# First mixer: SiLU from ScalarE's own table instead of tanh and a VectorE step, and a group's decay exponentials made together

## Chip, cores and metric

The kernel runs on one core of a Trainium2 chip. The metric is the device time of one execution in microseconds (us), the median of several runs. The engines are TensorE (PE in the profile; its weight loads are PEld), VectorE (DVE), ScalarE (ACT), GpSimd (POOL) and SyncE (SP), which issues the DMAs.

## What is computed

The reference is a chain of two transformer blocks over 272 (16 + 256), then 256 tokens with 1024 features. The change touches its first mixer alone, `ssd_mixer`: an input projection to 48 x 128 features, a causal convolution of four taps with SiLU, a chunked state recurrence for 8 groups of 4 heads over chunks of 16, 128 and 128 tokens, a gate by SiLU of `z`, a norm and an output projection:

```
z, xbc, dt = jnp.split(h @ w_in, ...)
xbc = jax.nn.silu(causal_depthwise_conv(xbc, conv_w, conv_b))
xs, b_in, c_in = jnp.split(xbc, ...)
...
decay = jnp.exp(jnp.where(causal, a_cs[..., :, None] - a_cs[..., None, :], -jnp.inf))
cb = jnp.einsum('bclgn,bcsgn->bcgls', c_c, b_c)
y_diag = jnp.einsum('bcgjls,bcsgjp->bclgjp', cb[:, :, :, None] * decay, xdt)
decay_to_end = jnp.exp(a_cs[..., -1:] - a_cs)
...
y_off = jnp.einsum('bclgn,bcgjpn->bclgjp', c_c, prev) * decay_from_start[..., None]
y = y + xs * d_skip
g = y * jax.nn.silu(z)
```

## The kernel before

All weights stream in through one ordered list of blocks, `PLAN`. A block is 128 output features: SP loads 512 KB into one of four `RAW` buffers, ACT rounds it to `WH` (`act_split`), DVE subtracts to get the remainder `WL` (`dve_split`), and PE multiplies with three matmuls for each of 8 chunks, 24 in all (`pe_block`). ACT makes `WH` three blocks ahead (`LEAD`), DVE makes `WL` two ahead (`LEAD_LO`).

The first mixer is the block "dt", then 48 blocks of the input projection, called block 0 to block 47 here, six to a group: two of x, one of b, one of c, two of z. Each engine runs a fixed, written-out program with a step for each block n, and executes it strictly in that order; only semaphores tie the engines together. In step n:

- ACT splits the weights of block n+3, starts the convolution of block n (`conv_base`, a scaled copy into `TMP`; not for z), and makes the tanh of block n-1, which waits for that block's third tap.
- DVE splits block n+2, makes the SiLU of block n-2 from its tanh (`dve_silu`, one scalar_tensor_tensor into `G6`), and adds the three taps of block n-1 (`dve_taps`).
- every engine then does its part of the recurrence (the "core") of the groups that are due: group g's core has 14 steps, and step k falls on n = 6g + 5 + k (`ssd_cores`).

In the core of group g, PE's `pe_prepare(g, i)` writes bank 3 for tile i: C.B, two transposes of x and, for the first two tiles, the transpose of B. DVE takes `xdt` from it, ACT copies the transposed B to `btk` (semaphore "bt"), and PE may write bank 3 again only after that: `pe_prepare(g, 1)` waits for the `btk` copy of tile 0. Then `act_prepare` makes the decays of the tile: an exponential of `ROWS` into `CE`, four Relu into `EE` (difference of two cumulated sums for each of four heads), and one exponential of `EE`. Tiles 0, 1 and 2 of group g are prepared in steps 6g+6, 6g+7 and 6g+10, and `pe_apply` uses them in steps 6g+8, 6g+10 and 6g+12. POOL multiplies `CE` with C. Step k = 12 of a group, two groups later in order, makes a logarithm and an exponential (`act_table`) and so loads another activation table.

PE's place in a bank is given back by the tap or, for a z block, by the SiLU of the block (`ssd_read`): block n waits for the reader of block n-3.

Of the kernel before, what the change touches and what calls it, by code (L numbers as in the profile page):

```python
# [5 lines left out]
ALU = mybir.AluOpType  # L6
# [5 lines left out]
T1 = 272  # L12
# [7 lines left out]
EXPS = "exp_and_others"  # L20

# [194 lines left out]
def build_program(nc, cpack, xin, memin, gains, W, out):  # L216
    with ExitStack() as ctx:
# [312 lines left out]
        EE = carve(2, 512)  # L530
        CE = carve(512)
        STA = carve(2, 256)

        ROWS = carve(2, 4, T1)
        decay_rows = nc.dram_tensor("decay_rows", [32, T1], F32, kind="Internal").ap()
        s_scanned = sem("s_decay_rows_stored")
        s_rows = [sem("s_decay_rows0"), sem("s_decay_rows1")]
        halved = sig("conv_halved")
# [5 lines left out]
        ident, tap, tanh, silu = sig("conv_base"), sig("conv_tap"), sig("tanh"), sig("silu")  # L544
# [25 lines left out]
        def ssd_cores(n):  # L570

            c = [(g, n - 6 * g - 5) for g in range(8) if 1 <= n - 6 * g - 5 <= 14]
            return c[::-1] if n < 50 else c

        def ssd_tile(g, i):
            o, L = TILES[i]
            return o, L, (3 * g + i) % 2

# [21 lines left out]
        def pe_prepare(q, g, i):  # L600
# [17 lines left out]
        def pe_apply(q, g, i):  # L618
            o, L, z = ssd_tile(g, i)
            yb, sbk = banks[5], banks[6]  # L620
            E4 = EE[:, z, :].rearrange("p (h l) -> p h l", h=4)
# [8 lines left out]
            for h in range(4):  # L630
                o_ = yb[64 * (h % 2):64 * (h % 2) + 64, 128 * (h // 2):128 * (h // 2) + L]
                t = q.matmul(o_, xdt[0:L, z, 64 * h:64 * h + 64], E4[0:L, h, 0:L], True, i == 0)
                if i:
                    t = q.matmul(o_, STA[:, i - 1, 64 * h:64 * h + 64], CE[:, 128 * h:128 * h + 128], False, True)
# [86 lines left out]
        def act_dt_core(q, k):  # L721
# [7 lines left out]
            else:  # L729
                for i, (o, L) in enumerate(TILES):  # L730
                    q.activation(acs[0:L, i, :], b[0:L, 64 * i:64 * i + 32], ACT.Copy).then_inc(*dta("acs", i))
                q.activation(dec[:, :], b[:, 96:128], ACT.Exp).then_inc(*dta("dec"))
                for i in range(2):
                    L = TILES[i][1]
                    q.wait_ge(*dtd["to_end", i])
                    q.activation(dte[0:L, i, :], dte[0:L, i, :], ACT.Exp).then_inc(*dta("dte", i))

        def act_prepare(q, g, i):
            o, L, z = ssd_tile(g, i)
            b = banks[3]  # L740
            E4 = EE[:, z, :].rearrange("p (h l) -> p h l", h=4)
            A4 = ROWS[:, g % 2, :, o:o + L]
# [14 lines left out]
            p = before(g, i, 2)  # L757
            if p is not None:
                q.wait_ge(*yps[p])
            for h in range(4):  # L760
                t = q.activation(E4[0:L, h, 0:L], A4[0:L, h, :], ACT.Relu, -1.0, acs[0:L, i, 4 * g + h:4 * g + h + 1])
            t.then_inc(*rel(g, i))
            q.wait_ge(*rel[g, i])
            q.activation(E4[0:L, :, 0:L], E4[0:L, :, 0:L], ACT.Exp, -1.0).then_inc(*dexp(g, i))

        def act_ssd_core(q, g, k):
            s = g % 2
            key = ("ssd", g)
            if k == 1:
# [9 lines left out]
            elif k == 5:  # L779
                act_prepare(q, g, 2)  # L780
# [28 lines left out]
        def act_ssd(q):  # L809
# [8 lines left out]
            for n in range(48):  # L818
                act_block(q, "ssd", 0, n, T1)
                if n % 6 < 4:  # L820
                    ch = ssd_channel(n)
                    q.wait_ge(*halved["b"])
# [53 lines left out]
        def dve_dt_core(q, k):  # L876
# [6 lines left out]
            else:  # L883
                q.wait_ge(*dta["dec"])
# [31 lines left out]
        def dve_weigh(q, g, i):  # L916
            o, L, z = ssd_tile(g, i)
            E4 = EE[:, z, :].rearrange("p (h l) -> p h l", h=4)
            q.wait_ge(*dexp[g, i])
# [2539 lines left out]
```

## Time and profile before

| what | value |
|---|---|
| median of 3 runs | 1629.4 us (1629.14 to 1630.18) |
| profiled execution | 1627.8 us |
| its span, first to last instruction | 1625.9 us |
| PE busy | 1604.5 us, 99% of the span |
| DVE busy | 1149.4 us, 71% |
| ACT busy | 963.5 us, 59% |
| POOL busy | 320.7 us, 20% |
| DMA | 161 GB/s in the mean |

The profiled execution's time is 1.9 us more than its span. Busy shares are means over stages; the first mixer lies between 11 us and about 255 us of the span. Matmuls are pipelined: a row's duration overlaps the next one's, so the distance between two starts tells the pace.

### The profile page before, as it was taken

The page shows a single profiled execution, that of the slowest core. Times are in us where ns is not written, and L with a number is a line of the kernel's source. Part 1 is how long each engine was busy: PE and PEld are TensorE (multiplying, and loading weights), DVE is VectorE, ACT ScalarE, POOL GpSimd, SP SyncE. Part 2 cuts the span into 40 slices and gives each one's busy share as a digit, 9 for nine tenths or more (in the row PEclk, how much of TensorE's full clock was granted, in tenths as well). Part 3 has the DMA queues.
Part 4 walks back from the last instruction along what each step waited for, and adds up shares of the span by engine and source line. Part 5 has one row for each costly group of instructions (what it writes and reads, how often), then busy time and mean ns, then how long its engine had stood idle before and what let it go on. Part 6 is the DMA issues. An engine that isn't in the chain of part 4 may idle for free.

```text
span 1625.9 us, 31615 instructions
## 1 busy us (share of the span) xinstructions
PE 1604.5 (99%) x12696; PEld 1545.1 (95%) x12696; DVE 1149.4 (71%) x1965; ACT 963.5 (59%) x1753; POOL 320.7 (20%) x291
## 2 busy tenths in 40 slices
PE   7999999999999999999999999999999999999998
PEld 7999999999998899999999999999999999999997
DVE  7999987555578765556776756766688767785655
ACT  7788876544456755544766645544466765664444
POOL 0001002234442232336311201000240111100000
PEclk9999999999999999999999999999999999999999
DMA  6544445555532356556545544555564445455553
GB/s 218 174 157 131 158 139 160 180 171 170 180 104 86 98 183 195 183 182 192 156 141 170 171 127 159 179 174 181 178 195 152 142 137 158 121 166 184 182 191 118
DMA packets 75792, 261.81 MB, mean 161 GB/s; under 512 B 8416, under 2 KB 11904, under 8 KB 75520
## 3 DMA queue, kind: packets, MB, share of 16 engines
q1 hardware_dynamic: 75648, 259.80, 51.1%
q8 instruction: 101, 1.65, 0.4%
q14 instruction: 43, 0.35, 0.1%
HBM read 258.68 MB, written 1.08 MB: 160 GB/s over the span
## 4 chain that ended last, share of the span: by engine, by line
PE 87%; DVE 5%; ACT 3%; issue 2%; POOL 2%; DMA 0%; DVEq 0%; SPq 0%; POOLq 0%; ACTq 0%
PE pb L156 86%; PE pb L159 2%; DVE WL L175 1%; POOL X L175 1%; DVE SCR L187 1%; DVE TMP L187 1%; ACT SCR L166 1%; ACT WH L165 1%; POOL SQ L175 1%; ACT HNH L165 0%; DVE SCR L175 0%; POOL SCR L175 0%; DVE HNL L187 0%; ACT SQ L165 0%; DVE MX L196 0%
## 5 line engine op out<-in xcount | busy, mean ns | idle before, releaser
L175 DVE TENSOR_TENSOR WL<-RAW,WH 128x1024 fp32r<-128x1024 f32 (+4 forms) x504 | 598.1, 1191 | 9.5 <-ACT WH L165 9.2
L165 ACT ACTIVATE WH<-RAW 128x1024 fp32r<-128x1024 f32 (+4 forms) x504 | 504.9, 1004 | 135.7 <-PE pb L156 135.2
L156 PE MATMUL pb<-HNH,WH 128*128 128x256 f32 (+1 forms) x1992 | 576.2, 289 | 1.5 <-issue 1.1
L156 PE MATMUL pb<-HNH,WL 128*128 128x256 f32 (+1 forms) x1992 | 564.8, 284 | 0.0
L156 PE MATMUL pb<-HNL,WH 128*128 128x256 f32 (+1 forms) x1992 | 564.6, 283 | 0.0
L156 PE MATMUL pb<-ASH,WH 128*128 128x256 f32 (+2 forms) x1392 | 400.3, 288 | 2.8 <-DVE WL L175 2.5
L156 PE MATMUL pb<-ASH,WL 128*128 128x256 f32 (+2 forms) x1392 | 394.9, 284 | 0.0
L156 PE MATMUL pb<-ASL,WH 128*128 128x256 f32 (+2 forms) x1392 | 394.3, 283 | 0.0
L156 PEld LDWEIGHTS pb<-HNH,WH 128*128 128x128 f32 x1992 | 375.7, 189 | 8.3 <-issue 3.2
L156 PEld LDWEIGHTS pb<-HNL,WH 128*128 128x128 f32 x1992 | 374.8, 188 | 2.0
L156 PEld LDWEIGHTS pb<-HNH,WL 128*128 128x128 f32 x1992 | 376.2, 189 | 0.0
L156 PEld LDWEIGHTS pb<-ASH,WH 128*128 128x128 f32 (+1 forms) x1392 | 261.9, 188 | 7.5 <-issue 5.1
L156 PEld LDWEIGHTS pb<-ASH,WL 128*128 128x128 f32 (+1 forms) x1392 | 262.1, 188 | 0.1
L156 PEld LDWEIGHTS pb<-ASL,WH 128*128 128x128 f32 (+1 forms) x1392 | 261.3, 188 | 0.7
L175 POOL TENSOR_TENSOR SQ<-SQ 128x256 f32<-128x256 f32 (+1 forms) x64 | 82.1, 1283 | 236.5 <-ACT SQ L165 236.3
L175 DVE TENSOR_TENSOR ASL<-TMP,ASH 128x256 fp32r<-128x256 f32 (+1 forms) x108 | 46.5, 430 | 108.8 <-ACT ASH L165 108.7
L156 PE MATMUL pb<-SCR 128*64 128x128 f32 (+10 forms) x880 | 119.3, 314 | 0.9 <-DVE SCR L187 0.8
L165 ACT ACTIVATE ASH<-TMP 128x256 fp32r<-128x256 f32 (+1 forms) x108 | 45.6, 422 | 114.6 <-DVE TMP L175 65.0
L175 POOL TENSOR_TENSOR X<-X,TMP 128x272 f32<-128x272 f32 (+1 forms) x64 | 96.3, 1505 | 79.5 <-DVE TMP L175 79.5
L156 PEld LDWEIGHTS pb<-SCR 128*64 128x64 f32 (+4 forms) x880 | 89.4, 160 | 20.4 <-issue 8.4
L175 POOL TENSOR_TENSOR SCR<-SCR 128x512 f32<-128x512 f32 (+2 forms) x36 | 44.6, 1247 | 310.9 <-DVE SCR L187 180.4
L165 ACT ACTIVATE TMP<-TMP 128x256 f32<-128x256 f32 (+1 forms) x84 | 35.4, 422 | 112.3 <-DVE TMP L187 111.9
(170 smaller groups left out, 1888.0 us busy)
## 6 DMA issues: line engine op xcount, KB each, us to landing
RAW<-in_w_gu SPq DMA_DIRECT2D x88, 512.0 KB, 4.2
RAW<-in_w_up SPq DMA_DIRECT2D x64, 512.0 KB, 3.7
RAW<-in_w_down SPq DMA_DIRECT2D x64, 512.0 KB, 3.6
RAW<-in_w_ssd SPq DMA_DIRECT2D x48, 512.0 KB, 3.6
RAW<-in_w_xkv SPq DMA_DIRECT2D x32, 512.0 KB, 4.2
RAW<-in_w_mlin SPq DMA_DIRECT2D x24, 512.0 KB, 3.6
RAW<-in_w_sbqkv SPq DMA_DIRECT2D x24, 512.0 KB, 3.6
RAW<-in_w_fd SPq DMA_DIRECT2D x22, 512.0 KB, 3.5
```

The costliest lines, as they stand in the source:

```text
L156: return self.eng.matmul(o, l, r, start=start, stop=stop, skip_group_check=skip) if self.eng else Nothing()
L159: return self.eng.transpose(o, i, ident) if self.eng else Nothing()
L165: return self.eng.activation(o, i, f, bias=bias, scale=scale)
L166: return self.eng.activation(o, i, f, bias=bias, scale=scale, accum_out=accum)
L175: return self.eng.tensor_tensor(o, a, b, op) if self.eng else Nothing()
L187: return self.eng.scalar_tensor_tensor(out=o, in0=a, scalar=s, in1=b, op0=op0, op1=op1)
```

## The change

SiLU is taken from ScalarE's Silu function, straight into `G6`. The tanh, the DVE step, the halving of the convolution's weights on POOL and the factor 0.5 at the gate go. The Relu go ahead of them: for g > 0 tile 1 in step k = -2 and tiles 0 and 2 in step k = -1, for g = 0 all three in step k = 0. For g = 0 the exponentials of `dec` and `dte` move there too, from step 3. `CE` and `EE` have two copies (by group parity), `ROWS` only one. POOL's products for both long tiles wait for a tap of block 6g+7.

```
         def ssd_cores(n):
-            c = [(g, n - 6 * g - 5) for g in range(8) if 1 <= n - 6 * g - 5 <= 14]
+            c = [(g, n - 6 * g - 5) for g in range(8) if -2 <= n - 6 * g - 5 <= 14]
...
         def pe_prepare(q, g, i):
-                q.wait_ge(*dta["dec"])
+                q.wait_ge(*dta["dec_log"])
...
         def act_prepare(q, g, i):
...
                 q.activation(btk[0:L, i, :], b[0:L, 384:512], ACT.Copy).then_inc(*btkd(g, i))
-            if i == 0:
-                q.wait_ge(s_rows[g % 2], 16 * (g // 2 + 1))
-            if i:
-                p = (g, 1) if i == 2 else (g - 1, 2)
-                if p[0] >= 0:
-                    q.wait_ge(*yps[p])
-                q.activation(CE[:, :].rearrange("p (h l) -> p h l", h=4), A4, ACT.Exp).then_inc(*cex(g, i))
...
-            q.wait_ge(*rel[g, i])
-            q.activation(E4[0:L, :, 0:L], E4[0:L, :, 0:L], ACT.Exp, -1.0).then_inc(*dexp(g, i))
+        def act_relu(q, g, i):
+            o, L = TILES[i]
+            q.wait_ge(s_rows, 16 * (g + 1))
+            if g > 1:
+                q.wait_ge(*yps[g - 2, i])
+            for h in range(4):
+                t = q.activation(decay(g, i)[:, h, :], ROWS[0:L, h, o:o + L], ACT.Relu, -1.0,
+                                 acs[0:L, i, 4 * g + h:4 * g + h + 1])
+            t.then_inc(*rel(g, i))
+        def act_decays(q, g):
+            q.table(LOGS)
+            if not g:
+                q.wait_ge(*dta["dec_log"])
+                q.activation(dec[:, :], dec[:, :], ACT.Exp).then_inc(*dta("dec"))
+                for i in range(2):
+                    L = TILES[i][1]
+                    q.wait_ge(*dtd["to_end", i])
+                    q.activation(dte[0:L, i, :], dte[0:L, i, :], ACT.Exp).then_inc(*dta("dte", i))
+            q.activation(CE[:, g % 2, :, :], ROWS[:, :, NMETA:T1], ACT.Exp).then_inc(*cex(g))
+            q.wait_ge(*rel[g, 0])
+            q.activation(decay(g, 0), decay(g, 0), ACT.Exp, -1.0).then_inc(*dexp(g, 0))
+            q.wait_ge(*rel[g, 2])
+            e = EE[:, g % 2, :, :]
+            q.activation(e, e, ACT.Exp, -1.0).then_inc(*dexp(g, 1))
...
         def act_ssd_core(q, g, k):
-            if k == 1:
+            if k == -2 and g:
+                act_relu(q, g, 1)
+            elif k == -1 and g:
+                act_relu(q, g, 0)
+                act_relu(q, g, 2)
+            elif k == 0:
+                if not g:
+                    for i in (1, 0, 2):
+                        act_relu(q, g, i)
+                act_decays(q, g)
+            elif k == 1:
                 act_prepare(q, g, 0)
...
         def act_ssd_item(q, n):
-            if n >= 2:
-                q.wait_ge(*silu[n - 2])
-            q.table(EXPS)
-            d = TMP[:, 3 + n % 2, 0:T1]
+            q.table(SILU)
+            if n >= 18:
+                q.wait_ge(*gated[n // 6 - 3])
             if n % 6 < 4:
                 q.wait_ge(*tap[n, 2])
-                q.activation(d, TMP[:, n % 3, 0:T1], ACT.Tanh).then_inc(*tanh(n))
+                v = TMP[:, n % 3, 0:T1]
             else:
                 q.wait_ge(*ssd_ready(n))
-                q.activation(d, ssd_source(n), ACT.Tanh, 0.5).then_inc(*tanh(n))
+                v = ssd_source(n)
+            q.activation(G6[:, n // 6 % 3, n % 6, :], v, ACT.Silu).then_inc(*silu(n))
...
-        def dve_silu(q, n):
-            q.stt(G6[:, n // 6 % 3, n % 6, :], TMP[:, 3 + n % 2, 0:T1], 1.0, v, ALU.add, ALU.mult).then_inc(*silu(n))
...
         def pool_ssd(q):
-            q.ts(cc("convw"), cc("convw"), 0.5, ALU.mult).then_inc(*halved("w"))
-            q.ts(cc("convb"), cc("convb"), 0.5, ALU.mult).then_inc(*halved("b"))
...
         def sync_rows(q, g):
-            if g < 2:
+            if g:
+                q.wait_ge(*cex[g - 1])
+            else:
                 q.wait_ge(s_scanned, 16)
-            else:
-                q.wait_ge(*rel[g - 2, 2])
```

The first place is ACT in steps 4 to 6, up to the `btk` copy of group 0's tile 0 (`SCR<-pb 16x128`). Names: `WH<-RAW` is a weight split, `TMP<-pb,cp` a `conv_base`, `TMP<-TMP` and `TMP<-SCR` a tanh. ACT before:

```order
L165 ACTIVATE WH<-RAW 128x1024 [waits block_done,s_raw0]
L165 ACTIVATE TMP<-TMP 128x272 [waits conv_tap,silu]
L165 ACTIVATE WH<-RAW 128x1024 [waits block_done,s_raw1]
L165 ACTIVATE TMP<-SCR 128x272 [waits evicted_dve,silu]
L165 ACTIVATE WH<-RAW 128x1024 [waits block_done,s_raw2]
L165 ACTIVATE TMP<-pb,cp 128x272 [waits silu,block_done]
L165 ACTIVATE TMP<-SCR 128x272 [waits evicted_dve]
L165 ACTIVATE SCR<-pb 16x128 [waits spare_state_rows,xdt]
```

ACT now, from the silu of block 3 to the same copy (the split and the silu of block 4 ahead of the Relu are left out here; they stand as before):

```order
L166 ACTIVATE SCR<-SCR 128x128 [waits s_decay_rows]
L166 ACTIVATE SCR<-SCR 128x128 x3
L166 ACTIVATE SCR<-SCR 16x16 x4
L166 ACTIVATE SCR<-SCR 128x128 x4
L173 ACT_TABLE_LOAD
L166 ACTIVATE SCR<-SCR 128x32 [waits dt_act]
L166 ACTIVATE SCR<-SCR 16x32 [waits dt_dve]
L166 ACTIVATE SCR<-SCR 128x32 [waits dt_dve]
L166 ACTIVATE SCR<-SCR 128x1024
L166 ACTIVATE SCR<-SCR 16x64 [waits decay_relu]
L166 ACTIVATE SCR<-SCR 128x1024 [waits decay_relu]
```

```order
L166 ACTIVATE WH<-RAW 128x1024 [waits block_done,s_raw2]
L166 ACTIVATE TMP<-pb,cp 128x272 [waits silu,block_done]
L173 ACT_TABLE_LOAD
L166 ACTIVATE SCR<-SCR 128x272 [waits evicted_dve]
L166 ACTIVATE SCR<-pb 16x128 [waits spare_state_rows,xdt]
```

Twelve Relu, six exponentials and two table loads now stand ahead of the copy, between the tanh (now silu) of block 4 and it.

The second place is ACT in the same two steps of a later group (g >= 2). Before:

```order
L165 ACTIVATE WH<-RAW 128x1024 [waits block_done,s_raw1]
L165 ACTIVATE TMP<-pb 128x272 [waits silu]
L172 ACT_TABLE_LOAD
L165 ACTIVATE Rbuf<-pb,cp 128x272 [waits squares_summed]
L165 ACTIVATE Rbuf<-Rbuf 128x272 [waits ln_of_sum]
L165 ACTIVATE WH<-RAW 128x1024 [waits block_done,s_raw2]
L165 ACTIVATE TMP<-pb,cp 128x272 [waits silu,block_done]
L172 ACT_TABLE_LOAD
L165 ACTIVATE TMP<-pb 128x272
L165 ACTIVATE SCR<-pb 16x128 [waits xdt]
```

Now:

```order
L166 ACTIVATE SCR<-pb 128x272
L173 ACT_TABLE_LOAD
L166 ACTIVATE SCR<-SCR 128x1024
L166 ACTIVATE SCR<-SCR 16x64 [waits decay_relu]
L166 ACTIVATE SCR<-SCR 128x1024 [waits decay_relu]
L166 ACTIVATE Rbuf<-pb,cp 128x272 [waits squares_summed]
L166 ACTIVATE Rbuf<-Rbuf 128x272 [waits ln_of_sum]
L166 ACTIVATE WH<-RAW 128x1024 [waits block_done,s_raw2]
L166 ACTIVATE TMP<-pb,cp 128x272 [waits silu,block_done]
L173 ACT_TABLE_LOAD
L166 ACTIVATE SCR<-pb 128x272
L166 ACTIVATE SCR<-pb 16x128 [waits xdt]
```

Here only the three exponentials came in between; the Relu stand one and two steps earlier, and the two table loads were there before.

The third place is what PE waits for at the beginning of group 0's core; its rows are the same before and now but for line numbers. `SCR 128x128 [waits bt]` is `pe_prepare(0, 1)`, after block 7:

```order
L156 MATMUL pb<-SCR 16x16 [waits silu,dt_act,dt_dve]
L159 MATMUL pb<-cp,SCR 16x128 x3
L156 MATMUL pb<-HNH,WH 128x272 [waits w_low,evicted_dve]
...
L156 MATMUL pb<-SCR 128x128 [waits bt]
L159 MATMUL pb<-cp,SCR 128x128 x3
L156 MATMUL pb<-HNH,WH 128x272 [waits w_low,evicted_dve]
```

Nothing moved on PE.

## Rows read from the trace of the kernel before

**Rows 1.** The page's busy line, and PE's waits from 10 to 60 us.

```profile
PE 1604.5 (99%) x12696; PEld 1545.1 (95%) x12696; DVE 1149.4 (71%) x1965; ACT 963.5 (59%) x1753; POOL 320.7 (20%) x291
...
PE pb L156 <- DVE WL L175: 1.1, 2, 0.7
PE pb L156 <- ACT SCR L165: 0.6, 1, 0.6
```

**Rows 2.** Timeline of PE, blocks 6 to 8: start, duration, idle before.

```profile
38.09 0.36 PE L156 MATMUL pb<-HNH,WH 128*128 128x272 f32 x1 [1.10 <-issue]
...
42.15 0.20 PE L156 MATMUL pb<-SCR 128*16 128x16 f32 x2 [0.81 <-DVE SCR L187]
...
42.54 0.37 PE L156 MATMUL pb<-HNH,WH 128*128 128x272 f32 x1
...
45.52 0.29 PE L156 MATMUL pb<-HNH,WL 128*128 128x272 f32 x1
45.64 0.38 PE L156 MATMUL pb<-SCR 128*128 128x128 f32 x2
...
46.11 0.37 PE L156 MATMUL pb<-HNH,WH 128*128 128x272 f32 x1
```

**Rows 3.** Timeline of PE around the preparation of tile 1, groups 4 and 5.

```profile
143.18 0.29 PE L156 MATMUL pb<-HNH,WL 128*128 128x272 f32 x1
...
143.89 0.39 PE L156 MATMUL pb<-HNH,WH 128*128 128x272 f32 x1
...
167.93 0.29 PE L156 MATMUL pb<-HNH,WL 128*128 128x272 f32 x1
...
168.93 0.39 PE L156 MATMUL pb<-HNH,WH 128*128 128x272 f32 x1
```

**Rows 4.** Timeline of DVE, steps 4 and 31.

```profile
38.27 0.42 DVE L187 SCALAR_TENSOR_TENSOR SCR<-TMP 128x272 f32<-128x272 f32 x1
38.62 1.55 DVE L187 SCALAR_TENSOR_TENSOR TMP<-SCR,cp,TMP 128x269 f32<-128x269 f32 x3
...
143.41 0.43 DVE L187 SCALAR_TENSOR_TENSOR SCR<-TMP,pb 128x272 f32<-128x272 f32 x1
```

**Rows 5.** Timeline of ACT, steps 4 to 7 and 29 to 30.

```profile
40.26 0.43 ACT L165 ACTIVATE TMP<-TMP 128x272 f32<-128x272 f32 x1 [2.18 <-DVE TMP L187]
...
43.93 0.27 ACT L165 ACTIVATE SCR<-pb 16x128 f32<-16x128 f32 x1 [0.23 <-DVE SCR L175]
44.10 1.18 ACT L165 ACTIVATE SCR<-SCR 16x16 f32<-16x16 f32 x5
...
48.16 2.46 ACT L165 ACTIVATE SCR<-SCR 128x512 f32<-128x512 f32 x6
...
137.57 1.28 ACT L172 ACT_TABLE_LOAD   x1
138.87 0.49 ACT L165 ACTIVATE Rbuf<-pb,cp 128x272 f32<-128x272 f32 x1
...
142.84 0.25 ACT L165 ACTIVATE SCR<-pb 16x128 f32<-16x128 f32 x1
```

**Rows 6.** Groups of ACT from 40 to 245 us, by shape: count, busy, mean ns.

```profile
L165 ACT ACTIVATE WH<-RAW 128x1024 fp32r<-128x1024 f32 x52 | 54.4, 1046 | 0.5 <-PE pb L156 0.5
...
L165 ACT ACTIVATE SCR<-SCR 128x512 f32<-128x512 f32 x32 | 20.1, 629 | 4.4 <-PE pb L156 3.9
L172 ACT ACT_TABLE_LOAD x13 | 16.7, 1283 | 0.2
```

**Rows 7.** PE's groups in 0:9 and 9.3:11.1; windows at the end, with PEclk.

```profile
L156 PE MATMUL pb<-SQ,cp 128*128 128x272 f32 x8 | 3.8, 662 | 5.4 <-ACT SQ L165 5.4
...
L156 PE MATMUL pb<-SQ,cp 128*128 128x272 f32 x8 | 2.1, 401 | 0.0
...
1619.50:1623.40 3.90, 0.00 (x0) 0.00 (x0) 2.80 (x8) 0.92 (x4) 0.00 (x0) 1.00 0.29 108
1623.60:1625.90 2.30, 0.00 (x0) 0.00 (x0) 0.00 (x0) 0.00 (x0) 0.00 (x0) 0.50 0.41 127
```

More of the change, by code:

```diff
@@ L20 @@
 EXPS = "exp_and_others"
+SILU = "silu_and_others"
 COLS = {}
@@ L529, in build_program @@
         btk = carve(2, 128)
-        EE = carve(2, 512)
-        CE = carve(512)
+        EE = carve(2, 2, 512)
+        E0 = carve(2, 64)
+        CE = carve(2, 4, T2)
         STA = carve(2, 256)
-        ROWS = carve(2, 4, T1)
+        ROWS = carve(4, T1)
         decay_rows = nc.dram_tensor("decay_rows", [32, T1], F32, kind="Internal").ap()
-        s_scanned = sem("s_decay_rows_stored")
-        s_rows = [sem("s_decay_rows0"), sem("s_decay_rows1")]
-        halved = sig("conv_halved")
+        s_scanned = sem("s_decay_stored")
+        s_rows = sem("s_decay_rows")
         spare = sig("spare_state_rows")
@@ L543, in build_program @@
         dtp = sig("dt_pe")
-        ident, tap, tanh, silu = sig("conv_base"), sig("conv_tap"), sig("tanh"), sig("silu")
+        ident, tap, silu = sig("conv_base"), sig("conv_tap"), sig("silu")
         prep_b = sig("prep_b")
@@ L577, in ssd_tile, with decay @@
             return o, L, (3 * g + i) % 2
+        def decay(g, i):
+            o, L = TILES[i]
+            a = EE[:, g % 2, i - 1, :] if i else E0[:, g % 2, :]
+            return a.rearrange("p (h l) -> p h l", h=4)[0:L]
         def before(g, i, n):
@@ L631, in pe_apply @@
                 o_ = yb[64 * (h % 2):64 * (h % 2) + 64, 128 * (h // 2):128 * (h // 2) + L]
-                t = q.matmul(o_, xdt[0:L, z, 64 * h:64 * h + 64], E4[0:L, h, 0:L], True, i == 0)
+                t = q.matmul(o_, xdt[0:L, z, 64 * h:64 * h + 64], E4[:, h, :], True, i == 0)
                 if i:
-                    t = q.matmul(o_, STA[:, i - 1, 64 * h:64 * h + 64], CE[:, 128 * h:128 * h + 128], False, True)
+                    t = q.matmul(o_, STA[:, i - 1, 64 * h:64 * h + 64], CE[:, g % 2, h, o - 16:o + 112], False, True)
             t.then_inc(*yps(g, i))
@@ L731, in act_dt_core @@
                     q.activation(acs[0:L, i, :], b[0:L, 64 * i:64 * i + 32], ACT.Copy).then_inc(*dta("acs", i))
[L732 to L736, printed above, removed]
+                q.activation(dec[:, :], b[:, 96:128], ACT.Copy).then_inc(*dta("dec_log"))
         def act_prepare(q, g, i):
@@ L749, in act_prepare @@
                 q.activation(btk[0:L, i, :], b[0:L, 384:512], ACT.Copy).then_inc(*btkd(g, i))
-            if i == 0:
-                q.wait_ge(s_rows[g % 2], 16 * (g // 2 + 1))
-            if i:
-                p = (g, 1) if i == 2 else (g - 1, 2)
-                if p[0] >= 0:
-                    q.wait_ge(*yps[p])
-                q.activation(CE[:, :].rearrange("p (h l) -> p h l", h=4), A4, ACT.Exp).then_inc(*cex(g, i))
-            p = before(g, i, 2)
-            if p is not None:
-                q.wait_ge(*yps[p])
+        def act_relu(q, g, i):
+            o, L = TILES[i]
+            q.wait_ge(s_rows, 16 * (g + 1))
+            if g > 1:
+                q.wait_ge(*yps[g - 2, i])
             for h in range(4):
-                t = q.activation(E4[0:L, h, 0:L], A4[0:L, h, :], ACT.Relu, -1.0, acs[0:L, i, 4 * g + h:4 * g + h + 1])
+                t = q.activation(decay(g, i)[:, h, :], ROWS[0:L, h, o:o + L], ACT.Relu, -1.0,
+                                 acs[0:L, i, 4 * g + h:4 * g + h + 1])
             t.then_inc(*rel(g, i))
-            q.wait_ge(*rel[g, i])
-            q.activation(E4[0:L, :, 0:L], E4[0:L, :, 0:L], ACT.Exp, -1.0).then_inc(*dexp(g, i))
+        def act_decays(q, g):
[13 more added lines that the diff above has]
+            q.activation(e, e, ACT.Exp, -1.0).then_inc(*dexp(g, 1))
         def act_ssd_core(q, g, k):
@@ L883, in dve_dt_core @@
             else:
-                q.wait_ge(*dta["dec"])
+                q.wait_ge(*dta["dec_log"])
                 for i in range(2):
@@ L1080, in pool_ssd @@
                         o, L = TILES[i]
-                        C4 = CE[:, :].rearrange("p (h l) -> p h l", h=4)
-                        q.wait_ge(*cex[g, i])
-                        if i == 1:
-                            q.wait_ge(*silu[6 * g + 6 if g < 7 else 47])
+                        C4 = CE[:, g % 2, :, o - 16:o + 112]
+                        q.wait_ge(*cex[g])
+                        q.wait_ge(*silu[6 * g + 3])
+                        if i == 1 and g < 7:
+                            q.wait_ge(*tap[6 * g + 7, 0])
                         q.tt(C4, C4, bc(G6[:, g % 3, 3, o:o + L], 4), ALU.mult).then_inc(*cem(g, i))
```

32 lines of the change are left out of this document (8 added, 24 removed).

## Prediction

> **What bounds the kernel now.** I read the page's busy line first: PE works 99% of the span [rows 1]. So the change can only help where PE waits inside the first mixer, and can only hurt where it makes a new wait there. PE's waits by releaser come next. From 10 to 60 us they add up to 3.6 us: 1.1 for `WL`, 0.6 for an ACT copy, 1.1 and 0.8 ahead of two matmuls [rows 1, 2]; from 60 to 250 us that view lists no wait of PE. The matmuls of the blocks follow each other every 0.13 us (24 starts from 42.54 to 45.52 [rows 2]), and that pace doesn't change. The whole prize is therefore below 0.3% of the time.
>
> The timeline of PE shows one more, small wait that the list hides. Between the last matmul of block 6g+7 and the first of block 6g+8 stands the preparation of tile 1. This distance is 0.59 us where nothing is late (45.52 to 46.11 [rows 2]), but 0.71 in group 4 and 1.00 in group 5 [rows 3]; over groups 1 to 7 it reads 0.59, 0.64, 0.71, 0.71, 1.00, 0.72 and 0.59, together 0.83 us too much. Block 32 needs the bank that the SiLU of block 29 reads; DVE makes it from 143.41 to 143.84, and PE goes on at 143.89 [rows 3, 4].
>
> Then the `btk` copy of ACT, which PE needs ahead of that same preparation. Group 0's runs at 43.93 and is needed at 45.64; group 4's ends at 143.09 and is needed at about 143.3 [rows 2, 3, 5]. It has little slack, and the change puts work ahead of it. That decides the case.
>
> **Edit by edit.**
>
> *DVE loses 48 SiLU steps.* One takes 0.35 us of DVE from start to start (38.27 to 38.62 [rows 4]), 17 us in all. DVE is what PE waits for up to 42 us, so here it counts: three of them stand ahead of the taps of block 3, which end at 38.62 + 1.55 = 40.17 [rows 4] and now at 39.1. The split that PE waits for at 38.09 comes 0.7 us earlier, and the wait of 0.81 us at 42.15, for the SiLU of block 3, goes, since ACT makes it right after the taps, at 39.2 to 39.6. Block 6 starts at 37.4, ends at about 40.5, and block 7 starts at 41.05 instead of 42.54: 1.5 us won. Block 7 then ends at 44.15.
>
> *The 0.83 us of groups 2 to 6* go too: the silu of block 6g+5 is now ACT's, some 2 us ahead of need (below). Later DVE work is hidden under PE anyway.
>
> *POOL's halving* is over long before the first convolution at 21 us; nothing. Its products with C move next to each other and now run beside DVE's taps; they were needed one step and more later, nothing.
>
> *SP.* The row load of group g > 0 waits for the `CE` exponential of the group before, and the weight loads queue behind it. The load is issued in the step where that exponential runs, so SP stands for 1 us or so; four `RAW` buffers are ahead. Nothing.
>
> *Silu for tanh on ACT.* No row shows Silu. Tanh takes 0.43 us for 272 columns [rows 5], a plain copy of a whole 1024 takes 1.05 [rows 6]; at worst it would cost like a second tanh, 0.35 us more a block. I take 0.43, since the functions in these rows are as quick as a copy of their size, and nothing makes this one another kind.
>
> *Group 0's burst.* Here is the price. All Relu and exponentials of group 0 now stand in step 5, ahead of the split, the convolution start, the second table load and the `btk` copy of step 6. Start to start, counted from the silu of block 3 at 39.2 (taps at 39.1 plus the 0.09 that the tanh at 40.26 came behind them [rows 4, 5]):
>
> - silu of block 3 0.35, split 0.95 (1.046 in [rows 6], less the 0.09 by which neighbours overlap), silu of block 4 0.35: 40.85;
> - eight Relu of 128 x 128. The tile at 48.16 takes 2.46 for a 512-column exponential, four Relu and a second exponential; with 0.63 for one of these [rows 5, 6] and the overlap, four Relu are 1.2, eight 2.4: 43.25;
> - four Relu and an exponential of 16 rows: the row of five, 1.18 less 0.1 [rows 5]: 44.35;
> - table load, 1.30 to the next start (137.57 to 138.87 [rows 5]): 45.65;
> - exponentials of `dec` and two `dte`, small, at most like those of the 16-row tile, 0.5 in all: 46.15;
> - two exponentials of 1024 columns, sized like the split, 0.95 each, and 0.1 to let the second end: 48.15;
> - step 6: split 0.95, convolution start 0.5, table load 1.3, silu of block 5 0.35, `btk` 0.25: 51.5.
>
> Before, this copy ended at 44.2. PE wants it at 44.15, waits until 51.5, and block 8 starts 0.47 later (45.64 to 46.11 [rows 2]), at 51.95 instead of 46.11: 5.8 us late, the 1.5 us included. Queued behind ACT in the meantime are DVE's `xdd` (it needs `dte`) and the `WL` of block 9 (its `WH` is done at 49.1, DVE at 50.3); PE needs that one at about 55.9, after block 8 and the first apply, so neither adds. ACT then has light steps, since the decays of tiles 1 and 2 are made, and is back with PE by block 10.
>
> *PE's clock.* 7.3 us of silence is long. At the end PE does nothing from 1619.5 on; the granted clock reads 1.00 until 1623.4 and 0.50 from 1623.6 [rows 7], that is 2.4 and 1.2 GHz, so it fell some 4 us after PE stopped. At the start the first eight matmuls of the sums, up to 9.0 us, take 662 ns in the mean and the next eight 401 [rows 7]; the first came at 5.40, so full clock took 3.6 us of work to come back. If the clock falls again at about 48.3, PE runs 3.6 us at half pace after 51.5 and loses 1.8 us. If it doesn't fall this is 0.
>
> *Later groups.* The first burst is special because ACT had no time to make the Relu ahead. For group 4 I follow ACT by the same slots from PE's end of block 27 at 126.2: convolution start, silu, four Relu (1.2), squares (0.64): 129; split, silu, Relu of two tiles (2.0): 132.3; split, silu of the z block: 133.5; table 134.8; three exponentials 137.0; logarithm and exponential 0.85: 137.8; split 138.8, convolution start (PE's block 30 ends at 138.4) 139.3, table 140.6, silu 140.9, copy 141.15. It was 143.09 and is needed at 143.3: 2.1 us of slack, more than before, because ACT no longer waits for a late DVE. The same holds for group 1 (without logarithm) from block 9 at 55.9. The change has four table loads more (two each in groups 0 and 1); those of group 1 fall into its slack.
>
> **The sum.** +5.8 (group 0) + 1.8 (clock) - 0.8 (late SiLU) = +6.8 us. After the mixer all engines follow PE, so it stays. Against the profiled execution 1627.8 + 6.8 = 1634.6; the median of the runs is 1.6 us above it, which gives 1636.2. A difference under 0.2%, 3.3 us, is about what can't be told from none.
>
> By the Trainium skill, "ScalarE: Activation LUTs", section "What ACT_TABLE_LOAD costs", a switch costs 2.66 us, the load and a drain of 1.38. Here 1.30 passes from the load's start to the next instruction [rows 5], with no idle time printed ahead of the load. By the page two loads ahead of `btk` would add 2.8 us in group 0, and in groups 2 to 7 the copy would end at 143.9, 0.6 late each; the sum would be +13.
>
> **Rivals.**
>
> - *The stall comes, the clock holds.* The only row of a fall is the end of the program, where other engines stop too. +5.0 us: 1634.4. 22%.
> - *Later groups stall as well,* because a table load drains first or ACT is some 2 us later than my slots, through `xdt`, `y_normed` or a slow Silu. With 2.1 us of slack in six groups, being 0.6 us over in each gives 3.6 us and, with 2.8 more in group 0, 13 us: 1642; with Silu at twice tanh's time, about 3 us more in each group uses the slack up and adds some 1 us in group 0: 1637 to 1640. For it: the slack was 0.2 before. Against it: the 1.30 row. 10%, of which 3% for the load that drains.
> - *Not slower: the copy is in time.* The mechanism is group 0's burst alone. If the copy ended by 44.15 only the gains stayed, -2.3 us: 1627.1. It decides at 46.4: there 0.8 us of the late `btk` cancels the 0.8 us of the silus. The burst would have to be 5.1 us shorter than its 12.3, for instance if 1024-column exponentials and Relu cost a third of their rows. For it speaks only that PE waited for nothing here before. 5%.
> - *The change doesn't ease DVE.* If the early wait at 38.09 is not DVE's split but what the row says, "issue", 0.7 us of the start's gain isn't there; the burst's end shifts by nothing, as the taps still lead. No change of the sum.
>
> **Numbers.** The forecast, stall and clock fall, 63%: 1635 to 1637.5. The range from 1633.4 to 1639.2 takes in the rival with the full clock, a burst 1 us off either way and part of the stalls of later groups. Slower by over 0.2% has 93%, within 0.2% 5% (copy in time, or half the burst), faster 2%.
>
> **What would show it.** In the trace after: PE idle of about 7 us behind ACT's copy near 44 to 51 us, ahead of the preparation of tile 1 of group 0; four table loads more in the mixer; matmuls of block 8 at twice the distance for some 3 us; block 6 starting at 37.4 and no wait ahead of the first preparation; all distances between blocks 6g+7 and 6g+8 at 0.59; DVE's busy time down by some 17 us. The prediction is wrong if ACT's burst runs faster than its parts, if Silu is slow, or if later groups show idle PE ahead of the same preparation.

## Result and the profile after

The changed kernel takes 1644.0 us (median of 4 runs, 1641.96 to 1644.88) against 1629.3 us for the kernel before in the same comparison (4 runs, 1628.19 to 1630.18): a ratio of 1.0091, with an interval of 1.0079 to 1.0103. It is 14.7 us slower, and lies outside the forecast's range of 1633.4 to 1639.2 us; the forecast was 6.8 us slower, 1636.2. Its profiled execution took 1643.2 us, with a span of 1641.4.

The page's busy line and the chain that ended last, after; they answer to [rows 1]:

```profile
PE 1608.6 (98%) x12696; PEld 1547.8 (94%) x12696; DVE 1139.0 (69%) x1917; ACT 964.6 (59%) x1742; POOL 322.4 (20%) x289
...
PE 79%; DVE 9%; ACT 6%; issue 3%; POOL 2%; DMA 0%; DVEq 0%; SPq 0%; POOLq 0%; ACTq 0%
```

DVE and ACT have together 9 us less to do than before, and yet their shares of the chain rose: before, it read PE 87%, DVE 5%, ACT 3%. PE's busy time grew by 4 us for the same 12696 matmuls; a part of them ran at the lower clock. What PE waits for in the kernel after, by releaser: total, times, longest, first from 10 to 60 us, then from 60 to 262 us:

```profile
PE pb L157 <- ACT SCR L166: 7.5, 2, 6.9
PE pb L157 <- DVE WL L176: 1.0, 2, 0.6
...
PE pb L157 <- ACT SQ L166: 4.9, 5, 1.0
PE pb L157 <- ACT SCR L166: 0.8, 4, 0.2
```

In the second stretch the kernel before had one wait, 0.3 us for `WL` at 255.34 us, behind the last group. One wait of 6.9 us was forecast; five waits of 1.0 us for `SQ` were not. Timeline of PE after (start, duration, what it is, idle before and its releaser), at the places that answer to [rows 2, 3]:

```profile
38.49 0.36 PE L157 MATMUL pb<-HNH,WH 128*128 128x272 f32 x1 [0.73 <-issue]
...
52.27 0.80 PE L157 MATMUL pb<-SCR 128*128 128x128 f32 x2 [6.93 <-ACT SCR L166]
...
53.36 0.57 PE L157 MATMUL pb<-HNH,WH 128*128 128x272 f32 x1
...
128.52 0.49 PE L157 MATMUL pb<-SCR 128*128 128x128 f32 x2 [0.19 <-ACT SCR L166]
...
129.09 0.37 PE L157 MATMUL pb<-HNH,WH 128*128 128x272 f32 x1
...
142.51 1.15 PE L157 MATMUL pb<-SQ,cp 128*128 128x272 f32 x4 [0.99 <-ACT SQ L166]
143.31 0.49 PE L157 MATMUL pb<-HNH,WH 128*128 128x272 f32 x1
```

The first three rows are group 0: block 6 at 38.49, PE idle until the `btk` copy, block 8 at 53.36 instead of 46.11. The rest repeats once a group: the preparation of tile 1 (block 26 follows at 129.09) and, three blocks later, the sums of a group's squares (block 29 at 143.31).

The loss follows from the starts of the blocks in both profiled executions, up to the last point of the mixer that can be named in both (255.34 us before, 270.68 after, 15.34 us apart). "Distance" is from the last block matmul ahead of the inserted work to the first one behind it.

All in us:

| where | before | after | lost |
|---|---|---|---|
| start of block 0 (clock rose at 11.4 instead of 9.0 us) | 14.76 | 15.93 | 1.17, chance |
| from there to the start of block 8 | 31.35 | 37.43 | 6.08 |
| block 8 to block 9 | 3.88 | 4.98 | 1.10 |
| group sums, blocks 6g+4 to 6g+5, five groups | 3.01 to 3.02 | 4.20 to 4.23 | 6.0 |
| preparation of tile 1, groups 2 to 6 | 0.64 to 1.00 | 0.72 to 1.06 | 1.1 |

The 1.17 us are called chance because block 0 starts anywhere from 14.73 to 15.93 us in the profiled executions of all kernels here, whose matmuls up to it are the same. Group 0 costs 7.2 us with the clock in it. The other half, 7.1 us, lies in the later groups, where the forecast had a gain of 0.8.

### The profile page after: what moved, and what is told of

It is laid out like the page before. It is cut to its first block, busy times and chain, and to the rows that moved or that the text cites. A ratio compares the mean times of both kernels' runs of the same rounds, so it can differ in the third digit from the quotient of the medians.

```text
span 1641.4 us, 31531 instructions
## 1 busy us (share of the span) xinstructions
PE 1608.6 (98%) x12696; PEld 1547.8 (94%) x12696; DVE 1139.0 (69%) x1917; ACT 964.6 (59%) x1742; POOL 322.4 (20%) x289
## 3 DMA queue, kind: packets, MB, share of 16 engines
q8 instruction: 101, 1.65, 0.4%
## 4 chain that ended last, share of the span: by engine, by line
PE 79%; DVE 9%; ACT 6%; issue 3%; POOL 2%; DMA 0%; DVEq 0%; SPq 0%; POOLq 0%; ACTq 0%
PE pb L157 78%; DVE WL L176 3%; ACT SCR L166 2%; DVE TMP L188 2%; DVE SCR L176 1%; PE pb L160 1%; ACT WH L166 1%; POOL X L176 1%; DVE SCR L188 1%; ACT L173 1%; ACT SCR L167 1%; POOL SQ L176 1%; ACT SQ L166 1%; ACT HNH L166 0%; ACT Rbuf L166 0%
## 5 line engine op out<-in xcount | busy, mean ns | idle before, releaser
L176 DVE TENSOR_TENSOR TMP<-pb,Rbuf 128x256 f32<-128x256 f32 (+1 forms) x89 | 38.2, 429 | 77.0 <-PE pb L157 77.0
```

The costliest lines, as they stand in the source:

```text
L176: return self.eng.tensor_tensor(o, a, b, op) if self.eng else Nothing()
```

## Why the group sums wait

The sums need the squares of a finished group. ACT makes them in step 6g+9, right behind the activation of block 6g+8 (tanh before, silu after), which waits for VectorE's third tap. ACT before, in step 27, at the tanh of block 26:

```profile
127.57 0.57 ACT L165 ACTIVATE TMP<-pb,cp 128x272 f32<-128x272 f32 x1
130.50 0.43 ACT L165 ACTIVATE TMP<-TMP 128x272 f32<-128x272 f32 x1 [2.36 <-DVE TMP L187]
130.84 0.73 ACT L165 ACTIVATE SQ<-SCR 128x272 f32<-128x272 f32 x2
```

PE's sums came at 131.44, right behind the first of these squares (131.25): there was hardly any slack before either. The same place after, now with the four Relu of tile 1 between the two:

```profile
136.72 0.57 ACT L166 ACTIVATE TMP<-pb,cp 128x272 f32<-128x272 f32 x1
...
140.45 0.43 ACT L166 ACTIVATE SCR<-TMP 128x272 f32<-128x272 f32 x1 [3.16 <-DVE TMP L188]
140.79 1.26 ACT L166 ACTIVATE SCR<-SCR 128x128 f32<-128x128 f32 x4
141.96 0.73 ACT L166 ACTIVATE SQ<-SCR 128x272 f32<-128x272 f32 x2
```

The Relu put the squares 1.17 us (140.79 to 141.96) behind where they were, and PE waits 0.99. And ACT still stands waiting for the tap, longer than before. VectorE lost three SiLU steps of 0.35 us on the way to that tap, and the tap is as late: 7.42 us behind the start of the block that follows it before (130.47, block 27 at 123.05), 7.44 after (140.41, 132.97). Timeline of DVE ahead of this tap, first before, then after:

```profile
124.42 1.56 DVE L187 SCALAR_TENSOR_TENSOR TMP<-pb,cp,TMP 128x269 f32<-128x269 f32 x3
125.90 0.69 DVE L175 TENSOR_TENSOR SCR<-SCR 128x512 f32<-128x512 f32 x1
...
126.78 0.72 DVE L187 SCALAR_TENSOR_TENSOR SCR<-SCR 128x544 f32<-128x544 f32 x1
```

```profile
133.57 1.56 DVE L188 SCALAR_TENSOR_TENSOR TMP<-pb,cp,TMP 128x269 f32<-128x269 f32 x3
135.04 1.02 DVE L176 TENSOR_TENSOR SCR<-SCR 128x512 f32<-128x512 f32 x1
...
136.28 1.53 DVE L176 TENSOR_TENSOR SCR<-SCR 128x544 f32<-128x544 f32 x1
```

And POOL after, in the same stretch; the two products of `CE` with C now run one behind the other:

```profile
134.23 2.99 POOL L176 TENSOR_TENSOR SCR<-SCR 128x512 f32<-128x512 f32 x2 [23.25 <-DVE TMP L188]
```

The decay product of DVE takes 1.02 us instead of 0.69 beside it and the gate 1.53 instead of 0.72: 1.14 us more, against 1.05 us for three SiLU steps that went. The taps, which read PSUM, take 1.56 in both. A third thing is smaller: the three exponentials of `act_decays` stand ahead of ACT's `Rbuf` rows, and VectorE now waits for those.

```profile
125.22 0.44 DVE L188 SCALAR_TENSOR_TENSOR TMP<-pb,Rbuf 128x272 f32<-128x272 f32 x1 [0.21 <-ACT Rbuf L166]
```

Counted from PE's preparation of tile 0 (113.78 before, 123.39 after), the taps of block 26 start 15.12 us later before and 15.47 after; PE itself loses 0.34 us in that stretch, ahead of block 26. By the Trainium skill, "SBUF — State Buffer", section "Who interferes with whom", a VectorE instruction with two SBUF inputs contends with a GpSimd instruction that reads SBUF, and one with a single SBUF input, outside the two-port modes, doesn't. The trace agrees in which instructions slow down: 0.72 to 1.53 us for the gate, 1.56 in both for the taps.

From the tap on, ACT has no gap up to group 4's `btk` copy, which is over at 154.7; PE needs it 0.2 us earlier.

## Experiments

All times are medians, each against the kernel before, measured beside it (1628.2 to 1629.1 us there). The kernel after stands at +14.7. Differences of 1 us between medians are near what chance makes here: the start of block 0 moves by up to 1.2 us, and the granted clock can fall once more long after the mixer (last section).

**Squares ahead of the Relu.** Inside a step, ACT does the squares first.

```
-                for g, k in ssd_cores(n):
+                for g, k in sorted(ssd_cores(n), key=lambda c: c[1] == -2):
```

> Only the order on ScalarE in step 6g+9 changes: the two squares of group g-1 ahead of the four Relu of group g+1's tile 1. Theory A (chain): ScalarE has no idle time between the late third tap that it waits for (140.41 us for group 4) and the btk copy (154.7), so the squares come in time, TensorE's waits of 1.0 us ahead of the group sums go, and the same time comes back as a longer wait for the btk copy of tile 0 of the next group: 1644 us, within 1 us of the changed kernel. Theory B (local): the Relu ahead of the squares are the whole cost of the later groups; the waits ahead of the sums go and nothing comes back: 1638 us, 6 us less.

Measured: 1644.4 us (1642.61 to 1644.87), ratio 1.0095 (1.0078 to 1.0111). Nothing is won, as the chain theory said. PE's waits from 60 to 262 us:

```profile
PE pb L157 <- ACT SCR L166: 6.3, 5, 1.4
```

The waits for `SQ` are gone and have come back, whole, at the `btk` copy three steps later (distance 2.22 instead of 1.05). So the four Relu delay an ACT chain without slack that PE waits for at two places; their order in it doesn't matter.

**Relu into ACT's idle time.** The Relu of all later groups stand ahead of the activation that waits for the tap.

```
+                for g, k in ssd_cores(n):
+                    if k < 0:
+                        act_ssd_core(q, g, k)
                 if n:
                     act_ssd_item(q, n - 1)
                 for g, k in ssd_cores(n):
-                    act_ssd_core(q, g, k)
+                    if k >= 0:
+                        act_ssd_core(q, g, k)
```

> Steps k = -2 and -1 of a group (its twelve Relu) are put ahead of the silu of the step, so that ScalarE makes them while it waits for VectorE's third tap. Theory A (chain): 1.2 us of the chain after the tap are gone in each of the five groups with waits, the waits ahead of the group sums go, those for the btk copy stay about as they are: 1638 us, 6 us less than the changed kernel. Theory B (local): the same 6 us. A third theory, that the taps are late because of ScalarE's convolution start and move with it, expects nothing: 1644 us.

Measured: 1638.1 us (1636.38 to 1638.63), ratio 1.0053 (1.0038 to 1.0068), 5.9 us less than the kernel after. The waits at the sums are gone, and from 60 to 262 us PE waits 0.8 us in all.

**POOL's products apart.** Tile 2's product waits for a tap of the next block; before the change it ran later still, 9.9 us behind tile 1's (124.65 and 134.56).

```
-                        if i == 1 and g < 7:
-                            q.wait_ge(*tap[6 * g + 7, 0])
+                        if g < 7:
+                            q.wait_ge(*tap[6 * g + 6 + i, 0])
```

> GpSimd's second product of a group waits for the first tap of block 6g+8 instead of starting right behind the first product. Theory A: the two products side by side lengthen VectorE's decay product from 0.69 to 1.02 us and its gate from 0.72 to 1.53 ahead of the late tap; with the second product moved away the tap comes about 0.8 us earlier, and so everything behind it: 4 us less in five groups, 1640 us. If the tap is late for other reasons (its release by TensorE's preparation alone) nothing moves: 1644 us.

Measured: 1639.9 us (1639.49 to 1640.11), ratio 1.0066 (1.0051 to 1.0081), 4.1 us less than the kernel after, by moving work on an engine that is busy 20% of the time. The gate of DVE in this run, and PE's waits from 60 to 262 us:

```profile
135.02 0.72 DVE L176 TENSOR_TENSOR SCR<-SCR 128x544 f32<-128x544 f32 x1
```

```profile
PE pb L157 <- ACT SQ L166: 1.0, 5, 0.3
PE pb L157 <- ACT SCR L166: 0.8, 4, 0.2
```

The gate is back at 0.72 us, the tap 0.8 us earlier, and the distance at the sums is 3.40 instead of 4.21. So the contention on DVE was a cause, not a companion.

**Group 0's copy first.** The Relu and exponentials of group 0 stand behind its `btk` copy.

```
             elif k == 0:
-                if not g:
-                    for i in (1, 0, 2):
-                        act_relu(q, g, i)
-                act_decays(q, g)
+                if g:
+                    act_decays(q, g)
             elif k == 1:
                 act_prepare(q, g, 0)
+                if not g:
+                    for i in (1, 0, 2):
+                        act_relu(q, g, i)
+                    act_decays(q, g)
```

> Group 0's Relu and exponentials stand behind the btk copy of its tile 0 (step 6) instead of in step 5. My theory of the first stall: the wait of 6.93 us ahead of the preparation of tile 1 goes; TensorE instead waits some 3.5 us ahead of the first apply, for the decays of tile 0; the clock stays at 2.4 GHz or nearly so; 5 us less than the changed kernel: 1639 us. If the stall is due to something else in step 6 (the weight split, xdt), it stays: 1644 us.

Measured: 1639.7 us (1639.23 to 1640.88), ratio 1.0066 (1.0051 to 1.0081), 4.3 us less than the kernel after. Timeline of PE, and its windows with the granted clock (the last column but two):

```profile
51.17 1.76 PE L157 MATMUL pb<-SCR 16*64 16x16 f32 x10 [3.00 <-DVE SCR L176]
```

```profile
48.00:50.00 2.00, 0.17 (x2) 1.00 0.03 13
50.00:52.00 2.00, 0.83 (x9) 0.53 0.79 269
52.00:54.00 2.00, 2.00 (x8) 0.50 0.64 259
...
56.00:58.00 2.00, 2.00 (x14) 0.77 0.06 23
```

The wait of 6.9 us is gone and one of 3.0 has come, ahead of the first apply, which needs the weighed decays (3.5 were expected). The later groups are as in the kernel after (distances 4.20 to 4.24). The expectation that the clock holds was wrong: a wait of 3.0 us was enough for it to fall, at 50.1, 1.9 us after PE stopped at 48.2, and it stayed low until 56.9 (0.77 in the mean of the last window).

**One table.** Tanh from the table that also holds exp, in the place of Silu, so that the decays need no load. The gates then hold a tanh: this kernel leaves the SiLU out, and serves for its time alone.

```
-SILU = "silu_and_others"
+SILU = "exp_and_others"
...
-            q.table(LOGS)
+            q.table(EXPS)
...
-            q.activation(G6[:, n // 6 % 3, n % 6, :], v, ACT.Silu).then_inc(*silu(n))
+            q.activation(G6[:, n // 6 % 3, n % 6, :], v, ACT.Tanh).then_inc(*silu(n))
```

> The function Silu is replaced by Tanh of the same argument (so the gates are wrong: silu is not computed), and silu and decays both use the table set with tanh and exponential. Nothing else moves. This takes away the two table loads between the silu of block 3 and the btk copy of group 0, and the two of group 1; from group 2 on the two loads of each group stay, for the logarithm. Chain theory: group 0's stall gets 2.6 us shorter (6.93 to 4.3), the later groups keep their waits of 1.2 us: 1641.4 us, or 1640.3 if the clock then holds at 2.4 GHz. Rival: a Silu instruction, or the table of Silu, is what costs; then the later groups lose their waits too: 1635 us.

Measured: 1640.5 us (1639.76 to 1641.64), ratio 1.0072 (1.0059 to 1.0086), 3.5 us less than the kernel after. Group 0's wait is 4.09 us instead of 6.93, two loads less, and the five waits of 1.0 us are untouched. So neither Silu nor its table makes those, and the rival of 1635 us is out. The clock didn't hold here either (0.50 from 46.4 to 53.2). Silu itself costs no more than tanh: 423 ns in the mean of 26 in the kernel after, where tanh took 428 of 24 before.

**A dead VectorE step.** The SiLU step's cost comes back on DVE ahead of the taps, with nothing that uses its result.

```
+            if n >= 2:
+                q.wait_ge(*silu[n - 2])
+                q.stt(TMP[:, 3 + n % 2, 0:T1], G6[:, (n - 2) // 6 % 3, (n - 2) % 6, :], 1.0,
+                      G6[:, (n - 2) // 6 % 3, (n - 2) % 6, :], ALU.add, ALU.mult)
```

> VectorE gets the removed step back as dead work: at the old place a scalar_tensor_tensor of 272 columns from G6 into an unused row, result unused. Chain theory: the three of them between TensorE's preparation of tile 0 and the late tap make that tap 1.05 us later in each of five groups, and the burst of group 0 starts 1.05 us later: 6.3 us more than the changed kernel, 1650 us. It would show that the removed VectorE steps were worth as much and that the change lost more than that elsewhere. Rival: VectorE is off the path now that TensorE waits for ScalarE: 1644 us.

Measured: 1652.4 us (1651.09 to 1653.16), ratio 1.0144 (1.013 to 1.0158), 8.4 us more than the kernel after; 6.3 were expected. PE's waits from 60 to 262 us, and its windows at the first of these waits:

```profile
PE pb L157 <- ACT SQ L166: 10.3, 5, 2.2
```

```profile
119.00:121.00 2.00, 1.36 (x5) 0.76 0.61 193
121.00:123.00 2.00, 2.00 (x9) 0.50 0.17 70
```

Each of the five waits grew from 1.0 to 2.0 us or a little over, the 1.05 us of three steps, and block 8 starts 38.49 us behind block 0 instead of 37.43: that is what was expected. Most of the rest is the clock: it fell at the first of the five waits, and block 23 took 4.39 us to the start of block 24 instead of 3.21; in group 0 it was low for 10.2 us instead of 6.8, and block 8 took 5.89 us instead of 4.98. The DVE work ahead of the tap does set the later groups' time.

**The Silu alone.** The kernel before with Silu on ACT and the DVE step gone; the decays stay where they were, so each of the three places in a group needs a load ahead of it and one behind.

```
         def act_prepare(q, g, i):
...
+            q.table(LOGS)
...
         def act_ssd_item(q, n):
...
+            q.table(SILU)
...
+            q.activation(G6[:, n // 6 % 3, n % 6, :], v, ACT.Silu).then_inc(*silu(n))
```

> One half of the change alone: the SiLU comes from Silu on ACT, and the decay exponentials stay where they were, a tile at a time. Each of the three places then needs a table load before it and one behind it, eight loads a group instead of two. In the kernel before ACT is busy 22.6 of 26.27 us in the period of a group (115.43 to 141.70), so 3.7 us are free; six more loads at 1.30 us are 7.8 us. If ACT becomes the bound, each of some seven groups takes 4.1 us longer: +29 us, about 1658 us. The rival says that the loads only fill the time in which ACT stands waiting for VectorE's taps (21 us in all between 60 and 240 us, 3 us a group), and that the saved VectorE work pays for the rest: below 1640 us.

Measured: 1661.2 us (1660.3 to 1663.17), ratio 1.0202 (1.0187 to 1.0217), +33 us. ACT's loads from 60 to 240 us (count, busy, mean ns, idle before):

```profile
L173 ACT ACT_TABLE_LOAD x47 | 60.3, 1283 | 0.8
```

It is 60 us of loads where the kernel before has 16.7, and ACT's idle time ahead of the taps' readers is down from 21.6 to 3.6 us. The period of 26.27 us in the expectation is the kernel after's; before, a group took 24.75 us (block 25 to block 31, 115.43 to 140.18) with ACT busy 21.10, which leaves the same 3.7 us free. Here a group takes 30.0 us (blocks 20 to 26), and ACT is busy 29.2 of them: 5.2 us more a group, 4.1 expected. The granted clock fell five times inside the mixer, which is in the 33 us. The rival, in which the loads only fill idle time, is out. ACT is the bound here.

**The decays alone.** The kernel after with tanh and the SiLU step of DVE as before; the decays made together.

```
-            q.table(LOGS)
+            q.table(EXPS)
...
-            q.table(SILU)
...
+            q.table(EXPS)
...
+                if n >= 2:
+                    dve_silu(q, n - 2)
                 if n >= 1:
                     dve_taps(q, n - 1)
```

> The other half alone: a group's exponentials made together as in the kernel after, but the SiLU from tanh and a VectorE step as before (tanh and exp share a table, so no loads are added). By the chain theory the VectorE steps are back ahead of the tap of block 6g+8, which the whole ACT chain of the step follows: against the kernel after it is the tanh run (-3.5 us) plus what the dead VectorE step cost (+8.4 us, of which 2 us hang on a clock fall), so 1646 to 1649 us, with some 2 us of wait ahead of each of the five group sums. If Silu and its loads were the cause of the later groups' waits, the waits would be gone and only group 0's burst left: about 1634 us.

Measured: 1648.3 us (1647.31 to 1649.31), ratio 1.0119 (1.0102 to 1.0136), +20 us, inside the interval expected. PE's waits from 60 to 262 us:

```profile
PE pb L157 <- ACT SQ L166: 10.3, 5, 2.1
```

So the loss in the later groups belongs to the decays made together (Relu in the wrong place, POOL's products side by side). Each half of the change alone costs more than both: the one needs the other's saving.

**All of it rearranged.** Relu of all groups into idle time, for group 0 all three tiles a step earlier than in the kernel after; `btk` ahead of the activation; group 0's exponentials a step later; POOL's products apart. The part of the edit that orders ACT's step:

```
+                for g, k in ssd_cores(n):
+                    if k < 0 or k == 1:
+                        act_ssd_core(q, g, k)
                 if n:
                     act_ssd_item(q, n - 1)
+                if n == 6:
+                    act_decays(q, 0)
                 for g, k in ssd_cores(n):
-                    act_ssd_core(q, g, k)
+                    if k >= 0 and k != 1:
+                        act_ssd_core(q, g, k)
```

> The change with ScalarE's order rearranged: Relu ahead of the silu of their step, for group 0 too (all three tiles in step 4); the btk copy of tile 0 ahead of the silu and of the table load; group 0's exponentials behind both; GpSimd's second product one step later. Chain theory: after 43 us no wait ahead of the group sums or the btk copy, all distances between blocks 6g+7 and 6g+8 at 0.59 us; for group 0 about 1.2 us of wait ahead of the first apply, no fall of the clock, block 9 at 49.8 us of a run that starts like the one before; 1628.2 us, 1 us below the kernel before. If the later groups have another limit behind the two found, 0.5 us or more a group stays: 1631 us and above.

Measured: 1627.1 us (1626.07 to 1628.17, 11 runs) against 1628.6 (15 runs), ratio 0.9988 (0.9979 to 0.9997). It beats both kernels, the one before by 0.12%. PE's waits from 10 to 60 us, then from 60 to 262:

```profile
PE pb L157 <- DVE WL L176: 1.0, 2, 0.6
PE pb L157 <- issue: 0.7, 1, 0.7
PE pb L157 <- DVE SCR L176: 0.6, 1, 0.6
PE pb L157 <- ACT SCR L166: 0.6, 1, 0.6
...
PE pb L157 <- DVE WL L176: 0.3, 1, 0.3
```

All distances at the sums are 2.99 and all at the preparations of tile 1 0.59 or 0.60. Block 8 starts 29.70 us behind block 0, 1.65 less than before: the gains that the prediction named for the start and for groups 2 to 6 are there once nothing new is late, less the one new wait of 0.6 us ahead of the first apply (1.2 were expected). In the profiled executions the mixer ends at 253.62 us instead of 255.34 although block 0 starts 0.34 us later: 2.1 us won. The two whole executions are still alike (1627.9 and 1627.8 us), because in this one the granted clock fell to 0.50 once more at 521.7 us, long after the mixer, and in the one before it didn't.

## Why the prediction was half right

**Group 0's burst: right.** Forecast: copy over at 51.5, block 8 at 51.95, 5.8 us. ACT after (compare [rows 5]):

```profile
40.26 0.43 ACT L166 ACTIVATE SCR<-TMP 128x272 f32<-128x272 f32 x1 [2.35 <-DVE TMP L188]
...
41.55 3.54 ACT L166 ACTIVATE SCR<-SCR 128x272 f32<-128x272 f32 x13
45.11 1.28 ACT L173 ACT_TABLE_LOAD   x1
46.40 2.51 ACT L166 ACTIVATE SCR<-SCR 128x32 f32<-128x32 f32 x6
...
50.33 1.28 ACT L173 ACT_TABLE_LOAD   x1
51.63 0.43 ACT L166 ACTIVATE SCR<-SCR 128x272 f32<-128x272 f32 x1
51.96 0.25 ACT L166 ACTIVATE SCR<-pb 16x128 f32<-16x128 f32 x1
```

The chain starts at 40.26 where 39.2 was worked out, 1.1 us later because the whole start is 1.17 us later, and the copy ends at 52.2. Silu to copy is 11.95 us here, 12.3 forecast.

**The start eased: right.** Without the 1.17 us block 6 starts at 37.3 (forecast 37.4) and block 7 at 40.9 (41.05); the wait of 0.81 us ahead of the first preparation is gone.

**The clock: right, and in two pieces.** 1.8 us were forecast. PE's windows after, with the granted clock:

```profile
46.00:48.00 2.00, 0.00 (x0) 1.00 0.19 78
48.00:49.00 1.00, 0.00 (x0) 0.99 0.28 39
49.00:51.00 2.00, 0.00 (x0) 0.50 0.73 257
...
53.00:55.00 2.00, 2.00 (x11) 0.50 0.45 174
...
56.00:58.00 2.00, 2.00 (x23) 1.00 0.46 121
```

It fell to 1.2 GHz at 49.0, 3.6 us after PE stopped at 45.3 behind block 7, and was back at 55.8, 3.5 us after PE went on. From 52.27 to 53.36 the preparation cost 1.09 us instead of 0.47, and block 8 cost 1.10 more: 1.7 us. Stall and clock of group 0 are 7.2 us against 7.6 forecast. That the clock's part fits this well is partly luck: with the same wait of 6.9 us ahead, block 8 cost 1.9 and 2.2 us more instead of 1.1 in the runs with POOL's products apart and with the Relu early. The first rival, in which the clock holds, is out.

**Silu as quick as tanh, 1.30 us a load: right.** No drain shows: ACT's next instruction starts 1.29 and 1.30 us after the loads at 45.11 and 50.33. The 2.66 us that the Trainium skill, "ScalarE: Activation LUTs", section "What ACT_TABLE_LOAD costs", gives for a switch isn't there: the measured 1.3 us decides.

**Later groups: the step that failed.** "For group 4 I follow ACT by the same slots from PE's end of block 27 at 126.2: convolution start, silu, four Relu (1.2), squares (0.64): 129", and "2.1 us of slack, more than before, because ACT no longer waits for a late DVE". The walk lets ACT's silu follow its convolution start without a wait. But it waits 3.2 us there, for the tap; before it waited 2.4. DVE isn't late by its amount of work alone: in the kernel after it stands idle for 2.2 us until PE's preparation of tile 0 releases it, and behind that stands the same row of work. The three steps saved on it, 1.05 us, went to the contention with POOL (1.14 us), whose products the prediction costed at "nothing". With the tap unchanged, the four Relu are 1.17 us on a chain whose end PE awaits: the squares first, of which the prediction never asked when PE needs them, then the copy, 0.2 us late instead of in time.

So the later groups cost 7.1 us, 6.0 at the group sums and 1.1 at the preparations of tile 1, where -0.8 was forecast; the rest of the sum stands. Two terms of the sum failed, then: the slack that the walk found, and the 0 us for POOL's products. The rival "later groups stall as well" named the right groups, but a stall at the `btk` copy and other causes (a drain, a slow Silu); its 0.6 us each was half of what came. That its 1642 us lies nearest to the measured 1644.0 is luck: 2.8 of the 6.4 us that it adds are a drain that isn't there.

**The side that it could be.** "The copy is in time" gave 1627.1 us, 2.3 less than the kernel before, for a kernel in which only the gains stay. The rearranged kernel comes near that case: 1627.1, but against 1628.6 beside it, so 1.5 us less, with a new wait of 0.6 us in group 0. The gains are as forecast in kind and about in size (1.65 and 0.8 us in the distances); that the two absolute numbers are equal is luck.

## What to carry to other kernels

Before a group of work is moved ahead of another on an engine, follow the engine from the point where it last *waited*, not from where it was last seen, and list each thing that is queued behind it up to the next wait, with the moment at which another engine needs it: here the squares had hardly any slack, and came to stand right behind the Relu. Work saved on an engine that is released by another's work arrives where it counts only if nothing else lengthens the way; two engines' elementwise work placed side by side can take it back. Idle time of an engine that waits is the place to put what was moved: the same Relu ahead of the wait cost nothing.

## What was not expected of the hardware

- A VectorE product with both inputs in SBUF slowed from 0.69 to 1.02 us, another from 0.72 to 1.53, while a POOL product of 128 x 512 ran; taps with an input in PSUM stayed at 1.56. With POOL's products apart the gate took 0.72 again; the product of 1.02, which the first POOL product still runs beside, stayed.
- The clock fell after shorter silences than the end of the program had shown (about 4 us): a wait of 3.0 us in the run with group 0's copy first, and one of 2.0 us in the two runs with the SiLU step on DVE. There only the first of five such waits did it. In the run with the decays alone it also fell at 30.9 us, with no wait over 0.63 us in the 9 us before.
- When it falls differs too with the same wait of 6.9 us: 3.6 us after PE stopped in the kernel after, 1.9 us in the run with POOL's products apart (stop at 44.2, fall at 46.1).
- How long the lower clock lasts differs between runs with the same wait ahead of it: in the run with the Relu early it was low for 10.2 us instead of 6.8, and block 8 took 6.04 us to the start of block 9 instead of 4.98. With the copy first the clock was back some 5.7 us after PE's restart at 51.2, in the kernel after 3.5.
- In the profiled executions of eight of the nine experiments (all but the squares first) the clock read 0.50 for 3.4 us once more, somewhere between 521 and 559 us, where PE works with no wait over 0.7 us. The executions before and after have no such fall, and from the end of the mixer to the last matmul they take 1363.5 and 1363.6 us against 1364.7 to 1365.4 in those eight. Why all this varies stays open.
